# Walking the columns of a 512-wide fp32r matmul from last to first, on both the moving and the accumulator side

## What is computed

```python
u = _rmsnorm(h, norm_mix_w[l])
proj = jnp.einsum('btd,de->bte', u, w_in[l])
...
h = h + jnp.einsum('btd,de->bte', mix, w_out[l])
u = _rmsnorm(h, norm_ffn_w[l])
hid = jax.nn.silu(jnp.einsum('btd,df->btf', u, w_ffn_gate[l])) * jnp.einsum('btd,df->btf', u, w_ffn_up[l])
h = h + jnp.einsum('btf,fd->btd', hid, w_ffn_down[l])
...
proj = h @ w_in
q, k, v, g = jnp.split(proj, 4, axis=-1)
...
return o @ w_out
```

## Time and profile before

| what | before |
|---|---|
| median of 3 runs | 2598.83 us (2597.77 to 2602.55) |
| profiled execution | span 2599.7 us; its own time is not listed apart from the three |
| mean granted TensorE clock | 0.995 |
| TensorE matmul busy | 2554.0 us |
| VectorE, ScalarE busy | 1803.6 us, 1154.6 us |
| bytes moved | 605.74 MB, 233 GB/s in the mean |

### The profile page before, as it was taken

How to read it: one execution, slowest core, us unless ns; L and a number is a source line. 1 busy time by engine, 2 the same in 40 slices (tenths; PEclk the granted TensorE clock), 3 DMA queues, 4 the chain that set the end, 5 groups by cost and what they waited for, 6 DMA issues and landing times.

```text
span 2599.7 us, 38429 instructions
## 1 busy us (share of the span) xinstructions
PE 2554.0 (98%) x14550; PEld 2156.5 (83%) x14550; DVE 1803.6 (69%) x2342; ACT 1154.6 (44%) x1475; POOL 0.2 (0%) x4
## 2 busy tenths in 40 slices
PE   8999999999999999999999999999999999999998
PEld 8977878778888888888888888899987778999886
DVE  6897676776667777777776666776786665545756
ACT  5454333445544544444443334333486344334642
POOL 0000000000000000000000000000000000000000
PEclk9999999999999999999999999999999999999999
DMA  6777676776768888888887777888845546675464
GB/s 212 247 236 247 210 249 216 255 255 211 251 227 271 270 276 276 270 272 278 277 276 250 251 253 258 280 275 275 257 138 189 186 159 181 185 230 178 137 215 143
DMA packets 317949, 605.74 MB, mean 233 GB/s; under 512 B 27742, under 2 KB 31844, under 8 KB 316140
## 3 DMA queue, kind: packets, MB, share of 16 engines
q1 hardware_dynamic: 301628, 571.59, 68.3%
q10 hardware_dynamic: 16176, 32.15, 3.6%
HBM read 593.03 MB, written 10.62 MB: 232 GB/s over the span
## 4 chain that ended last, share of the span: by engine, by line
PE 90%; DVE 4%; DMA 2%; ACT 2%; issue 2%; SPq 0%; ACTq 0%; DVEq 0%
PE bank L661 22%; PE bank L663 22%; PE bank L662 22%; PE bank L688 5%; PE bank L686 5%; PE bank L687 5%; DMA gemv_w<-in_w_mod 2%; PE bank L604 2%; PE bank L787 1%; DVE gemv_acc L1927 1%; DVE w_lo L1908 1%; DVE conv_out L2056 1%; ACT w_hi L1281 1%; PE bank L1120 1%; PE bank L813 0%
## 5 line engine op out<-in xcount | busy, mean ns | idle before, releaser
L1908 DVE TENSOR_TENSOR w_lo<-raw,w_hi 128x1024 fp32r<-128x1024 f32 x820 | 1001.7, 1223 | 725.9 <-ACT w_hi L1281 723.9
L1281 ACT CAST w_hi<-raw 128x1024 fp32r<-128x1024 f32 x820 | 859.3, 1049 | 1347.1 <-PE bank L663 1001.7
L661 PE MATMUL bank<-w_hi,u_hi 128*128 128x512 f32 x1216 | 491.9, 404 | 6.3 <-issue 3.8
L663 PE MATMUL bank<-w_hi,u_lo 128*128 128x512 f32 x1216 | 481.2, 396 | 0.0
L662 PE MATMUL bank<-w_lo,u_hi 128*128 128x512 f32 x1216 | 480.9, 395 | 0.0
L1927 DVE SCALAR_TENSOR_TENSOR gemv_acc<-gemv_w,small,gemv_acc 128x512 f32<-128x512 f32 x480 | 357.9, 746 | 23.2 <-DMA gemv_w<-in_w_mod 21.9
L661 PE MATMUL bank<-w_hi,s_hi 128*128 128x512 f32 x744 | 300.9, 404 | 1.3 <-DVE w_lo L1908 1.2
L663 PE MATMUL bank<-w_hi,s_lo 128*128 128x512 f32 x744 | 294.2, 395 | 0.0
L662 PE MATMUL bank<-w_lo,s_hi 128*128 128x512 f32 x744 | 294.2, 395 | 0.0
L688 PE MATMUL bank<-s_hi,w_lo 128*128 128x256 f32 x1024 | 290.1, 283 | 0.0
L687 PE MATMUL bank<-s_lo,w_hi 128*128 128x256 f32 x1024 | 289.5, 283 | 0.0
(11 more groups left out here) (362 smaller groups left out, 2882.6 us busy)
## 6 DMA issues: line engine op xcount, KB each, us to landing
gemv_w<-in_w_mod SPq DMA_DIRECT2D x384, 256.0 KB, 3.2
raw<-in_w_in SPq DMA_DIRECT2D x176, 512.0 KB, 4.5
raw<-in_a_w_in SPq DMA_DIRECT2D x128, 512.0 KB, 4.5
raw<-in_w_ffn_gate SPq DMA_DIRECT2D x88, 512.0 KB, 4.6
raw<-in_w_ffn_up SPq DMA_DIRECT2D x88, 512.0 KB, 4.4
raw<-in_w_ffn_down SPq DMA_DIRECT2D x88, 512.0 KB, 4.3
gemv_w<-in_kv_w_mod SPq DMA_DIRECT2D x128, 256.0 KB, 3.5
raw<-in_kv_w SPq DMA_DIRECT2D x64, 512.0 KB, 3.7
```

The source lines that it names most:

```text
L661: pe.matmul(o, xh, w_hi[:, s, t], start=(k == 0), stop=False)
L663: ins = pe.matmul(o, xl, w_hi[:, s, t], start=False, stop=(k == 2 * units - 1))
L1281: act.copy(w_hi[:, s], raw[:, s]).then_inc(hi_done, 1)
L1908: dve.tensor_tensor(w_lo[:, s], raw[:, s], w_hi[:, s].bitcast(F32), ALU.subtract).then_inc(lo_done, 1)
```

## The change

In both functions that run the 512-wide products, the moving operand and the accumulator get a step of -1 in their last dimension. The stationary operand, the order of the matmuls, the semaphores and everything on the other engines stay as they are. Column c of the weights is still added into column c of the bank. The lists of instructions of all five engines have the same rows in the same order before and after.

```diff
@@ rows_apart
-                        o = acc[x][th][:]
+                        o = acc[x][th][:, ::-1]
                         for t in range(2):
                             k = 2 * u + t
                             xh, xl = hi[:, k, th * P:(th + 1) * P], lo[:, k, th * P:(th + 1) * P]
-                            pe.matmul(o, xh, w_hi[:, s, t], start=(k == 0), stop=False)
-                            pe.matmul(o, xh, w_lo[:, s, t], start=False, stop=False)
-                            ins = pe.matmul(o, xl, w_hi[:, s, t], start=False, stop=(k == 2 * units - 1))
+                            pe.matmul(o, xh, w_hi[:, s, t, ::-1], start=(k == 0), stop=False)
+                            pe.matmul(o, xh, w_lo[:, s, t, ::-1], start=False, stop=False)
+                            ins = pe.matmul(o, xl, w_hi[:, s, t, ::-1], start=False, stop=(k == 2 * units - 1))
```

## The result

| what | before | after |
|---|---|---|
| median, 4 runs each | 2598.42 us (2597.77 to 2602.55) | 2607.89 us (2607.59 to 2611.73) |
| ratio | | 1.0038, 95% interval 1.0026 to 1.0050 |
| span of the profiled execution | 2599.7 us | 2605.7 us |
| mean granted clock | 0.995 | 0.997 |

The change costs 9.5 us, 0.38%. That is small, and about twice what a measurement of this kernel can tell from no change. A second measurement in the experiments gave 1.0040 (1.0027 to 1.0053). Two executions in the experiments, one of the write-alone kernel (5083.97 us) and one of the kernel before (7902.17 us), took about two and three times the usual time at a granted clock of 1.00, and no ratio counts them; what held them up is not known.

What follows compares the result with a forecast made beforehand. The prediction took TensorE's matmul steps, 232.3 ns per 512-wide matmul, to bound the kernel. Its terms, 0 + 0 + 0 against the profiled span of 2599.7 us, gave 2599 us, with a range of 2520 to 2750 us.

Steps and rivals of the forecast that it cites:

- likeliest case: Whole kernel: no measurable change, 2599 us, own range 2594 to 2604; chance of no change 0.64.
- rival 2: 512-wide matmuls slower by a little, shortfall doubled: 19 ns each, at most 148 us more, 2747 us; chance 0.11.
- The bound: Whole kernel: TensorE, busy 2554.0 of 2599.7 us, sets the time through the steps between its matmuls.
- The count: Lines L661 to L663 and their late-row copy: 7776 touched matmuls of 512 columns, filling 1806 us.
- The read: Moving operand w_hi or w_lo walked from column 511 to 0: as dense as before, so 0 us.
- The write: Accumulator bank written from column 511 to 0: same bounds as for reading, taken as 0 us.
- The adds: Three matmuls adding into one bank: a column is met again after 512 columns as before, no added wait.
- Rival 1: 512-wide matmuls: neighbouring columns no longer paired, 194 ns more each, 1506 us in all, 4105 us; chance 0.18.
- Rival 3: 512-wide matmuls: turning removes some of the shortfall, at most 148 us less, 2451 us; chance 0.07.
- The signs: Forecast wrong if the step at L661 to L663 moves over 1 ns; reason wrong if the 256-wide step moves.

## Why the prediction was right and where it failed

The range, 2520 to 2750 us, held the time, but it is wide and that says little. The likeliest case, no change within 0.2%, did not come: 2607.89 us is outside its own 2594 to 2604. What came is of the kind of rival 2, at 0.11, with a price of 9.5 us where that rival's was at most 148, and a step of 234.0 ns where it had 240 to 250. By the prediction's own sign, a step at L661 to L663 that moves by over 1 ns, the forecast of no change was wrong.

- **The bound.** Right. TensorE's steps are the time: in the profiled pair the terms of its steps sum to 7.6 us and its busy time rose by 7.3, and no other engine did more or longer work.
- **The count.** 7776 matmuls, right.
- **The read: "I take 0".** This is the step that failed. The reason given, that the order is as dense as before, does not suffice. Turning the order within 16 bytes is free (232.52 ns), but taking the groups of 16 bytes from last to first has the whole cost: 234.11 ns against 232.47. The Trainium skill (SBUF — State Buffer, the note on cachelines) says that accesses into the same 16-byte line run at full bandwidth: the run with the order turned inside the groups agrees, at 1.0005. The page says nothing on the order of the lines. The prediction also left out that a turned operand starts at another place, 60 bytes into a block of 64, and in the shifted kernel, where the operand starts 32 bytes into one, the step rose by 0.9 ns with everything forward.
- **The write: "I take 0".** Right, 0.9997. The reading of the Trainium skill (Advanced Engine Details and Errata, PSUM Cachelines) by which a step of -1 would count as non-contiguous is wrong for this write.
- **The adds.** That none comes too soon after the last one to the same place was argued only for streams that all walk one way. The run with one of three turned shows no such wait even where they walk against each other: its step rose by 0.70 ns, less than with all three turned.
- **Rival 1, columns come singly**, 4105 us: excluded. The step rose by 1.5 ns, not by 194.
- **Rival 2.** Its kind was right: a small price at the high clock. The argument against it was wrong: the step seemed hardly to change, because the timeline rounds to 10 ns. To the nanosecond it went through 228 to 241 ns in a fixed series, so the shortfall does change from matmul to matmul. What it depends on is not shown.
- **Rival 3, faster.** It did not come. But with the tiles moved the 256-wide step fell by 1.3 ns, so there was something to gain on that side, though not by turning. The argument that the 256-wide products show the same 0.444 ns a column was circular, since that figure had been worked out from both widths. It also rested on k2 alone: with the 120.0 ns of k3 and q3 the two equations give 0.439 ns a column and 7.7 ns a matmul.
- **The signs.** I had written that the reason is wrong if the 256-wide step moves too. It moved, by 0.5 ns. It moves between kernels whose 256-wide products nobody touched, from 118.68 to 119.22 in the table (one trace each), so it is no sign of a cost there. But it isn't free of the change either: all runs whose three reads go down in groups of 64 bytes or less have 118.68 to 118.70, the repeat of the change too, and all others with forward 256-wide products and unmoved tiles have 118.80 or more. The difference lies in the products that could run at 120.0 ns, k3 and q3 above all. That the pace of the stream ahead of them decides this is a guess.

What is shown: the cost is in the read of the moving operand, not in the write. It needs groups of 16 to 64 bytes taken from last to first, or tiles moved so that the operand starts off a multiple of 64 bytes (the tiles behind them moved too); within 16 bytes, and from 256 bytes up, the order is free. What is not shown is how much of the full reversal's cost is its order and how much its starting place. A run with the operand turned and the tiles moved, so that it starts at the edge of a block, would tell. Its 236.7 and 240.0 ns, a tenth of the blocks, did not come in the shifted kernel, which speaks for a part of the order. What stays open is why. No single rule tried explains the paces of groups of 8, 16 and 64 columns together with that of the shifted tiles. There is a hint in numbers that come back: 233.3, 236.7 and 240.0 ns for a 512-wide step are 560, 568 and 576 cycles of 2.4 GHz, eight apart, and 120.0 ns is 288. The first is 512 + 32 + 16 and the last 256 + 16 + 16, as if a cycle were lost for every 16 columns and 16 cycles for every matmul, and the forward stream at its best pace paid some 13 in place of the 16. This is arithmetic on the steps and not shown by a run that takes one of the two away.

## What to carry to other kernels

In a kernel that is one long stream of matmuls, 1 ns in the step is 8 us, so the address pattern and the place of the moving operand are worth a test, and the step must be read to the nanosecond from many starts, not from durations or from two rows. Reading a moving fp32r operand upward, from a multiple of 64 bytes, was the fastest for the 512-wide matmuls here; writing the accumulator in the other direction, or swapping large pieces on the read side, was free, so a kernel that needs columns mirrored can do it on the write side. A small effect that is argued away by symmetry should be priced from the shortfall that the trace already shows.

## What the runs showed of the hardware that was not expected

- At the high clock (granted 1.00) the stream falls into a repeating series of steps: seven steps of 228 to 241 ns forward; three of 233, 233 and 234 ns downward in v2, with stretches of 236.7 and of 240.0 ns elsewhere; two of 234 and 239 ns with groups of 16 columns down in ffn.
- The same 256-wide code has two paces, 118.7 and 120.0 ns, and k3 ran at 120.0 ns before and at 118.7 ns after without being touched; what decides which one it falls into is open.
- With `w_hi` and `w_lo` moved by 32 bytes and the tiles behind them by 64, the 512-wide step changed by +0.9 ns and the 256-wide step by -1.3 ns.
- Matmuls that add into the same bank from opposite ends cost nothing like a wait for the add: at most 0.7 ns a matmul.
